# Three bf16 pieces in place of two scaled fp16 pieces for the router's gates in a two-block transformer kernel

## The reference

```
top_s, pick = lax.top_k(cand_s, K)                  # K = 16, 8 heads: 128 picks a token
experts = jnp.take_along_axis(cand_i, pick, axis=-1)
gates = jax.nn.softmax(top_s, axis=-1)
a = jnp.einsum('cd,ced->ce', hc, w_u[ec]).astype(F32)
coef = (gc * jax.nn.gelu(a)).astype(dt)
return jnp.einsum('ce,ced->cd', coef, w_v[ec])
```

## Time and profile before

| | |
|---|---|
| median of 3 runs | 3216.54 us (3209.97, 3216.54, 3218.43) |
| the profiled execution | 3209.97 us, its span 3208.3 us |
| busy over the span | PE 94%, PEld 81%, DVE 67%, ACT 40%, POOL 5% |
| granted TensorE clock, mean | 0.979 of 2.4 GHz |
| batches of gates (first to last matmul) | 1872 to 3002 us of the span |

### The profile page before, as it was taken

How to read it: one execution, slowest core, us unless ns; L and a number is a source line. 1 busy time by engine, 2 the same in 40 slices (tenths; PEclk the granted TensorE clock), 3 DMA queues, 4 the chain that set the end, 5 groups by cost and what they waited for, 6 DMA issues and landing times. The chain is left out here.

```text
span 3208.3 us, 45990 instructions
## 1 busy us (share of the span) xinstructions
PE 3026.5 (94%) x17110; PEld 2595.2 (81%) x17110; DVE 2162.8 (67%) x2746; ACT 1269.7 (40%) x1461; POOL 153.2 (5%) x246
## 2 busy tenths in 40 slices
PE   6999899999898999889999999999999999999997
PEld 5888688887777888888888988887888878877785
DVE  5586566676676666467669768745885468888744
ACT  4343444443443333234433334444344433444343
POOL 0011001101011001010000000000000000000000
PEclk9999999999999999899999999999999999999998
DMA  7766377665568775107544444455445544445453
GB/s 284 274 218 233 138 256 251 247 250 196 178 228 289 270 280 215 53 10 253 183 148 161 163 157 176 178 195 184 161 180 183 194 173 170 178 164 183 170 194 120
DMA packets 99163, 620.55 MB, mean 193 GB/s; under 512 B 10992, under 2 KB 11120, under 8 KB 36208
## 3 DMA queue, kind: packets, MB, share of 16 engines
q1 hardware_dynamic: 70112, 509.88, 44.5%
q0 software_dynamic: 28944, 109.25, 9.4%
HBM read 616.99 MB, written 2.10 MB: 193 GB/s over the span
## 5 line engine op out<-in xcount | busy, mean ns | idle before, releaser
L1418 DVE TENSOR_TENSOR wl<-ring,wh 128x2048 fp32r<-128x2048 f32 x468 | 1065.9, 2278 | 706.9 <-ACT wh L909 427.2
L909 ACT ACTIVATE wh<-ring 128x2048 fp32r<-128x2048 f32 x468 | 892.8, 1908 | 1353.8 <-PE ps L493 672.0
L491 PE MATMUL ps<-hhl,wh 128*128 128x512 f32 x3200 | 1143.7, 401 | 23.6 <-DVE wl L1418 19.8
L493 PE MATMUL ps<-hhl,wl 128*128 128x256 f32 x3200 | 899.2, 281 | 0.0
L491 PEld LDWEIGHTS ps<-hhl,wh 128*128 128x128 f32 x3200 | 606.4, 189 | 166.6 <-DVE wl L1418 22.7
L493 PEld LDWEIGHTS ps<-hhl,wl 128*128 128x128 f32 x3200 | 609.8, 191 | 0.0
L478 PE MATMUL ps<-wh,hhl 128*128 128x512 f32 (+1 forms) x864 | 335.6, 388 | 17.2 <-DVE wl L1418 12.5
L480 PE MATMUL ps<-wh,hhl 128*128 128x512 f32 (+1 forms) x864 | 332.4, 385 | 0.0
L479 PE MATMUL ps<-wl,hhl 128*128 128x512 f32 (+1 forms) x864 | 332.4, 385 | 0.0
L1434 DVE SCALAR_TENSOR_TENSOR aring<-aring,BIG 128x1024 f32<-128x1024 f32 x192 | 234.1, 1220 | 41.3 <-DMA aring<-in_ada 39.8
L824 PE MATMUL ps<-wh,stage_h 128*128 128x512 f32 x768 | 205.6, 390 | 4.1 <-issue 2.0
(11 more groups left out here) (251 smaller groups left out, 3158.4 us busy)
## 6 DMA issues: line engine op xcount, KB each, us to landing
ring<-in_stream SPq DMA_DIRECT2D x480, 1024.0 KB, 4.8
aring<-in_ada POOLq DMA_DIRECT2D x192, 512.0 KB, 4.9
X<-in_x SPq DMA_DIRECT2D x1, 2048.0 KB, 11.7
BIG<-in_nbr_bias POOLq DMA_DIRECT2D x2, 1024.0 KB, 5.0
BIG<-in_g_post POOLq DMA_DIRECT2D x2, 1024.0 KB, 7.6
out<-X SPq DMA_DIRECT2D x2, 1024.0 KB, 4.0
BIG<-in_decays POOLq DMA_DIRECT2D x2, 768.0 KB, 5.4
BIG<-in_cond SPq DMA_DIRECT2D x1, 1024.0 KB, 13.8
```

Source lines behind the costliest of these rows:

```text
L491: mm(ps[:, 4 + c, :], wh[:, c % 2, w], hhl[:, k, :, :].rearrange("p a b -> p (a b)"), start=(k == 0), stop=False, skip_group_check=True)
L493: last = mm(ps[:, 4 + c, 0:SEQ], wl[:, c % 2, w], hh[:, k, :], start=False, stop=(k == KD - 1), skip_group_check=True)
L909: return nc.scalar.activation(o, i, func, **kw)
L1418: return tt(blocks(wl[:, c % 2, :], cols), blocks(ring[:, c, :], cols), blocks(wh[:, c % 2, :].bitcast(F32), cols), ALU.subtract)
```

## The change

The type of the one-hot matrices and pieces becomes bf16, the gate is cut into three pieces, and the scale is gone. `hot2`, `gate_parts` and the matmul's output grow by half. Cutting takes one more step, two strided subtractions. `table_rest` was padding of 2 KB a partition, about what `hot2` and `gate_parts` grow by.

```diff
-GATE_PARTS = 2
-GATE_SCALE = 2.0 ** 15
+GATE_PARTS = 3
...
-        hot1 = sb("hot1", [P, 2, BATCH, KEYS], F16)
-        hot2 = sb("hot2", [P, 2, GATE_PARTS, BATCH, PART], F16)
-        equal2 = sb("equal2", [P, 2, BATCH, PART], F16)
-        table_rest = sb("table_rest", [P, 512])
+        hot1 = sb("hot1", [P, 2, BATCH, KEYS], BF16)
+        hot2 = sb("hot2", [P, 2, GATE_PARTS, BATCH, PART], BF16)
+        equal2 = sb("equal2", [P, 2, BATCH, PART], BF16)
...
-        iota_row = sb("iota_row", [P, KEYS], F16)
-        gate_parts = sb("gate_parts", [P, SEQ * GATE_PARTS * 2], F16)
-        index = sb("index", [P, 2, SEQ, 2], F16)
+        iota_row = sb("iota_row", [P, KEYS], BF16)
+        gate_parts = sb("gate_parts", [P, SEQ * GATE_PARTS * 2], BF16)
+        index = sb("index", [P, 2, SEQ, 2], BF16)
...
-            st(ts(gate_at[:, :, 0, :, :], twice(ps[:, 2, 0:SEQ]), GATE_SCALE, None, ALU.mult))
+            st(v.tensor_copy(gate_at[:, :, 0, :, :], twice(ps[:, 2, 0:SEQ])))
             st(v.tensor_copy(index[:, :, :, :], ps[:, 0:2, 0:SEQ].unsqueeze(3).to_broadcast([P, 2, SEQ, 2])))
             st.done()
-            st(stt(of_batches(gate_left), of_batches(ps[:, 2, 0:SEQ]), GATE_SCALE, gate_at[:, :, 0, :, 0], ALU.mult, ALU.subtract))
+            st(tt(of_batches(gate_left), of_batches(ps[:, 2, 0:SEQ]), gate_at[:, :, 0, :, 0], ALU.subtract))
             st.done()
             st(v.tensor_copy(gate_at[:, :, 1, :, :], twice(gate_left)))
+            st.done()
+            for two in range(2):
+                st(tt(gate_at[:, :, 2, :, two], of_batches(gate_left), gate_at[:, :, 1, :, two], ALU.subtract))
             st.done()
...
-                stt(o, gsum[b], 1.0 / GATE_SCALE, o, ALU.mult, ALU.mult).then_inc(g_used, 1)
+                tt(o, o, gsum[b], ALU.mult).then_inc(g_used, 1)
```

More of the change, by code:

```diff
@@ L26 @@
 F32R = mybir.dt.float32r
-F16 = mybir.dt.float16
+BF16 = mybir.dt.bfloat16
 U32 = mybir.dt.uint32
```

## The result

The changed kernel takes 3233.33 us (median of 5 runs, 3231.47 to 3238.96); before takes 3217.01 us (median of 5, 3209.97 to 3219.44). The ratio is 1.0058, with a 95% interval of 1.0047 to 1.0070: slower, by 16.3 us between the medians, and by 15 to 23 us by the ratio. Fourteen executions of the changed kernel are on record, 3231.0 to 3240.2 us. The profiled ones are 3234.34 us (span 3232.7) and 3209.97 us (span 3208.3).

The account below looks back on a forecast made before the run. PE was taken to bound the steady stages, with DVE covered: 13.7 + 0.1 (first batch at half clock) + 0.9 + 1.0 = 15.7 us, on the 3216.5 us median 3232 us; range 3221 to 3246.

Parts of the forecast that it names:

- PE's columns, 13.7 us: 128 batches on PE: 32 more columns for each of eight matmuls, 0.107 us a batch; bounds 9.2 and 15.9 us.
- The rival with hidden columns: PE's batch: weight loads pace it and hide the extra columns, 3219 us, within the noise; chance 0.07.
- The weight loads: Beside the batch's matmuls on PE: said to start 0.027 us apart, quicker than the matmuls, and not to grow.
- the rule of the Trainium skill: PE's batch: a load takes 107 ns for 128 columns; as pace, sum 2.5 us, not 15.7; hidden columns' chance 0.07.
- The head of U1, 0.9 us: PE's wait for the first `hot2`: two new subtractions add 0.80 us and `hot2` 0.13.
- The seams, 1.0 us: PE's waits between stages U2 to V2: 0.19 us extra at most places, +0.40 at V2's start.
- DVE, +0.40 us a slot, covered: Steady slots: `hot2` +0.13 and reduce +0.27 us, hidden in DVE's waits, with 0.09 us left in U, 0.08 in V2.
- The working for U: U slots: 0.27 + 0.107 us come off DVE's 0.46 us wait ahead of `low`, leaving 0.09.
- What more DVE work would cost: All 128 slots: each 0.1 us of DVE work beyond the thin cover was said to cost 13 us.
- Slots of 5.99 us: Profile after: slots were to grow from 5.88 to 5.99 us, with PE still busy throughout.

Follow-up runs that it names:

- e2: The kernel before with a third piece of zeros written once, so PE's batch matmuls are 96 columns wide and DVE works as before; ratio to before 1.0049.
- e6: The kernel before with the batch's matmuls reading 128 columns, DVE's part as before; 3236.0 us in one execution, beside one of before at 3220.4.
- e1: The kernel before with bf16 in place of fp16 and nothing else; ratio to before 1.0005.
- e3: The changed kernel with PE's batch cut back to 64 columns, DVE still writing and summing three pieces; ratio to before 1.0013.
- e4: The changed kernel with one more DVE comparison of 256 elements a slot, into a tile nobody reads; ratio to before 1.0080, from two runs.

## Why the prediction was right, and where it wasn't

The direction, the range and the size stand: 3232 us predicted, 3233.3 measured. The size is in part luck, since the terms beneath it differ: the same sum put the profiled execution at 3225.7 us, and it took 3234.3.

- **PE's columns, 13.7 us: 12.0.** The starts of a batch's matmuls went from 29.1 to 42.5 ns apart (the first two from 40 to 53), the 13.3 ns of the working. But V2's slots grew by 0.094 us, not 0.107: only the seven gaps between eight matmuls grow, and the next fp32 matmul starts 0.03 us after the batch's last one in both kernels. 128 x 0.094 = 12.0 us. The rival with hidden columns falls with e2. The Trainium skill (TensorE: Matmul & The Clock Gate, Back-to-back issue gap) gives N/2.4 + 2.5 ns for an isolated matmul, as an estimate 29.2 and 42.5 ns for these widths, and the trace agrees. For a stream of weight loads and matmuls the same section of the Trainium skill has more, about 81 ns at 128 columns; e6's batches, with a load ahead of every matmul, have 56.0.
- **The weight loads.** The prediction read them as 0.027 us apart, quicker than the matmuls, and as not growing. By their starts only the first two are closer, 15 ns; the others are 29.1 ns apart before and 42.5 after, as the matmuls are, while each lasts 98 ns. So the loads follow the columns, and the rule of the Trainium skill (TensorE: Matmul & The Clock Gate, LDWEIGHTS), which the prediction kept as a rival, is near the duration of one load, 107 against 98 ns, but doesn't set the pace here.
- **Missing: the slow rhythm.** 84 steady U slots grew by 0.19 us where the columns account for 0.094: the other 0.095 make 8.0 us that no term had. e2 shows that PE's wider batch brings them; e1 and e3 show that neither type nor DVE's work is needed.
- **The head of U1, 0.9 us: 1.0**, in the wait of PE. Both durations in it, 0.79 for the subtractions and 558 ns, were as worked out.
- **The seams, 1.0 us: not confirmed.** The wait at V2's start went from 3.05 to 3.38 us where 0.40 was forecast. The waits that the prediction counts at the seams add up to 14.3 us before and 14.6 after; the sum of all seam slots is +0.8, but with shifts of over 1 us both ways from time at half clock.
- **DVE, +0.40 us a slot, covered: right.** 0.133 + 0.267, and e3 has V2 slots at 5.81 us with all of it. The working for U was good: 0.08 us is left ahead of `low`, where 0.09 was given.
- **What more DVE work would cost: wrong.** The step that failed is "each 0.1 us that DVE takes beyond this costs 128 x 0.1 = 13 us". It took the 0.08 to 0.09 us ahead of `low` for the reserve of the whole slot. In U, work ahead of the reduce goes into the wait for the batch, which the working left out; and `low` ends 2.0 us before the next unit's first fp32 matmul. In V2 the real reserve was 0.15 us, not 0.08: from the start of `gated` to that of `low` are 0.50 us in the changed kernel and 0.35 in e4, where nothing holds `low` back. What went beyond it, 0.04 us a slot in e4, was a backlog that PE met only at the end of the pass. e4 cost about 1 us where this step gives 14. Work put between the batch and `low` in U, such as a dearer reduce, wasn't tried.
- **Slots of 5.99 us** were forecast for the profile after; U has 6.07, V2 5.91, neither. V2's slots were 5.81 before, not 5.88; and the 5.4 us given for DVE's work in a slot is 5.2 by the two figures beside it. No term hangs on either.

Added up for the profiled pair, the 114 steady slots have 114 x 0.094 = 10.7 us from the columns and 8.0 from the rhythm, the seam slots 0.8, the head 1.0: the 20.5 us seen from the head of U1 on. The medians are 16.3 apart. Both kernels wander: before took 3210 to 3219 us in the first five runs and 3207.9 to 3232.8 in the 39 beside the experiments. The runs don't settle how much of the gap between 20.5 and 16.3 is the slow rhythm in other executions of before (e3 has 25 such slots with 64 columns), and how much is the rest of the kernel.

What stays open is the cause of the two rhythms. The runs show when they come, and that the slow one has three steps, not what in PE holds 6.7 ns a pair, nor why a batch leads to one or the other. It wasn't tried to restart PE in the quick one ahead of each unit.

## What to carry to other kernels

When PE is busy throughout a stage, price an addition to it by the columns, at the pace of its own rows, and then look after the fact at work that wasn't touched: a small matmul put between long streams can shift the pace of the streams themselves. A wait that a profile shows ahead of one instruction isn't the reserve of the engine; ask where in the cycle the added work goes, which waits lie behind it, and what a late result would hold up. A difference of a few units' pace between two profiles of one kernel tells what a single execution is worth, before terms of that size are read out of it.

## What the runs showed of the hardware

- A stream of fp32 matmuls of 512 and 256 columns in turn runs at 346.7 or at 353.3 ns a pair at full clock; the slow rhythm is a cycle of 361, 349 and 350 ns. One execution has units of both, and one rhythm can last over tens of units.
- A batch of 16-bit matmuls between units can change the rhythm. Quick units stayed quick behind 64 columns (325 of 325), mostly turned slow behind 96 (15 of 18), and alternated with slow ones behind 128. Behind 64 and 96 columns a slow unit that ended with the long step of the cycle was followed by a slow one (30 of 30 and 341 of 341), any other by a quick one (9 of 9 and 5 of 5).
- V2's streams, all of 512 columns, show no second rhythm: steady slots of 5.81, 5.91 and 6.00 us at 64, 96 and 128 columns in every profile, 0.094 us for each 32 columns.
- In batches of eight pairs of a weight load and a 16-bit matmul, matmuls start 29.1, 42.5 and 56.0 ns apart at 64, 96 and 128 columns (before, after, e6), and the loads of 98 ns keep the same distance.
- bf16 and fp16 cost the same on both engines: eight matmuls of 64 columns 0.41 us, DVE's operations on 256, 512 and 1024 elements 285, 426 and 685 ns in e1 against 284, 425 and 685 before.
